# Routing weights ahead of the low halves: reordering the approach to a mixture of experts

## The chip, the cores and the metric

The kernel runs on one core of one Trainium2 chip. The metric is the device time of one execution in microseconds (us), lower is better; it is given as the median of repeated runs. A profile is one execution recorded by the hardware profiler, with a time of its own.

## The reference, cut to what matters

A two-layer block (pooling mixer, sliding window attention, two feed-forward nets) is followed by a second block with attention, an mLSTM, a gating unit and then a hierarchical mixture of experts. The change lies where the second block's mixer ends and its experts begin. There the model has 256 tokens of width 1024, 32 experts in 4 groups and 2 experts for each token:

```
h = h + hierarchical_moe(rms_norm_2(h, norm2_g), ...)

g_logits = xt @ rg_w + rg_b;  g_top = argmax(g_logits);  g_w = softmax(g_logits)[g_top]
e_in = (xt @ re_w + re_b).reshape(-1, 4, 8)[g_top]
e_val, e_loc = top_k(e_in, 2);  e_w = softmax(e_val) * g_w
y = sum over the two chosen experts of e_w * ((silu(x @ w_gate[e]) * (x @ w_up[e])) @ w_down[e])

gate = sigmoid(rms_norm_2(h, ple_norm_g) @ ple_gate_w)
h = h + gate * (p @ ple_proj_w)
```

The product `p @ ple_proj_w` depends on nothing before it.

## The kernel before, in words

Every engine has its own hand-written instruction list, and the lists meet only at semaphores. An engine runs its list strictly in order, so an instruction that waits holds all that stands behind it. Activations lie transposed, 8 chunks of 128 channels by 256 tokens. Exact products of float32 are made from a high and a low half.

The stretch in question runs in this order:

1. **norm2.** ScalarE squares the 8 chunks of the residual `hs` (line 774, `square`), GpSimd adds the first seven up in `sqsum` (lines 623 and 627, `sum_chunks`), TensorE sums over partitions (line 1382), ScalarE makes the reciprocal root (lines 780 and 781) and VectorE writes the normed chunks into `mix` (line 2004). `square_at` says where a square is kept: for norm2 in `mix`, eight places, so that no square waits for a place. `sq` has four places, and there a square k waits until square k - 4 has been summed.
2. **Router.** TensorE makes the 36 logits of each token (line 1795) and transposes the normed tokens (line 1801). ScalarE copies the transposes out as the high halves `h2h` (line 1205), and later VectorE makes the low halves `h2l` from them (line 2121, four subtractions).
3. **Routing.** VectorE works through `routing` (lines 2092 to 2147): group, two experts of each token as one-hot rows, TensorE counts ranks with them (lines 1820 to 1824), and VectorE turns ranks into slots and slots into the selection matrix `psel[0]` (lines 2154 and 2157). The two softmaxes need an exponential each, made by ScalarE (lines 1208 and 1214); VectorE waits for both with `route_exp` and computes the weights w1 and w2 in five small operations (lines 2140 to 2144).
4. **The independent product.** TensorE makes the 8 chunks of `p @ ple_proj_w` (line 1813, `per_layer`) in two banks of PSUM that alternate. ScalarE copies each out (line 1211, into `ppT`), and TensorE may write chunk c only when chunk c - 2 has been copied. Two of the chunks stand ahead of the rank matmuls and six behind; the second exponential stands behind the second copy.
5. **Gathers.** TensorE gathers the tokens of a pair of teams by `psel` (lines 1832 and 1833, `gather`), ScalarE and VectorE copy the result out (lines 1220 and 2509, `gathered`) and only then gather(1) may begin, since it writes the same two banks.
6. **Spread.** GpSimd builds eight diagonal matrices `diag` (line 759) over the room of the weights of step 4, from the slots (pairs 0 and 2) and from w1 and w2 (pairs 1 and 3). TensorE spreads them over all partitions (line 1928), ScalarE copies (line 1241), and the experts begin.
7. **Experts.** 16 teams of two experts: gate and up (line 1860), a gather for two teams later, transposes, combination of the previous team (line 1883) and down (line 1874). The weights come through six slots of `wring`, each loaded again when TensorE has used it (line 564, on SyncE's queue).

`stay_busy` (line 1292) issues matmuls whose result nobody reads.

Of the kernel before, what the change touches and what calls it, by code (L numbers as in the profile page):

```python
# [9 lines left out]
ACT = mybir.ActivationFunctionType  # L10
ALU = mybir.AluOpType
AX = mybir.AxisListType
# [4 lines left out]
KD = D // P  # L17
# [70 lines left out]
NORM, SQ0 = {}, {}  # L88
# [72 lines left out]
def bass_two_blocks(nc, a, out):  # L161
# [4 lines left out]
    with ctx:  # L166
        def sb(name, shape, dt=F32, within=None):
            return (within or ctx).enter_context(nc.sbuf_tensor(name, shape, dt))
# [3 lines left out]
        def sem(name):  # L172
            if name not in sems:
                sems[name] = ctx.enter_context(nc.semaphore(name))
            return sems[name]
# [20 lines left out]
        mix = sb("mix", [P, KD, T])  # L196
        rstd = sb("rstd", [P, 2, T])
        sq = sb("sq", [P, 4, T])
# [11 lines left out]
        small = sb("small", [P, 420])  # L210
# [167 lines left out]
        def square_at(name, c):  # L378

            if name == "mixpost0":  # L380
                return gained[:, c, :]
            return mix[:, c, :] if name in ("mixpre0", "pre1", "norm1", "norm2", "ple") or name.startswith("ffnpre") else sq[:, (SQ0[name] + c) % 4, :]

        def r_of(name):
            return rstd[:, NORM[name] % 2, :]
# [25 lines left out]
        for part in SPLIT:  # L411
            if part in THIRD:
                k = 2
            elif part in FOURTH:
                k = 3
            else:
                k, turn_of = turn_of, 1 - turn_of
# [254 lines left out]
        def _(pool):  # L672
            chain = Chain(pool, "pool_chain")
# [78 lines left out]
            pool.wait_ge(sem("y_split"), 9)  # L752
            pool.memset(zero, 0.0).then_inc(sem("diag_ready"), 1)
            pool.wait_ge(sem("pp_psum"), KD)
            for known, pairs in ((1, ((0, 160), (2, 162))), (2, ((1, 164), (3, 166)))):
                pool.wait_ge(sem("columns_ready"), known)
                for i, col in pairs:
                    for b in range(NB):
                        pool.tensor_scalar(diag[:, 2 * i + b, :], ident, small[:, col + b:col + b + 1], None, ALU.mult)\
                            .then_inc(sem("diag_ready"), 1)  # L760
# [4 lines left out]
        def square(act, name, c, src, n, rows=P, **kw):  # L765

            k = SQ0[name] + c
            if k >= 4 and name not in ("mixpre0", "mixpost0", "pre1", "norm1", "norm2", "ple") and not name.startswith("ffnpre"):
                owner_, at = next((x, k - 4 - SQ0[x]) for x, m in NORMS if k - 4 - SQ0[x] < m)
                if at < SUMMED.get(owner_, 0):  # L770
                    act.wait_ge(sem("sq_summed"), sums(owner_, at))
                else:
                    act.wait_ge(sem("sq_used"), k - 3)
            act.activation(square_at(name, c)[0:rows, 0:n], src, ACT.Square, **kw).then_inc(sem("sq_ready"), 1)  # L774
# [173 lines left out]
        def _(act):  # L948
            chain = Chain(act, "act_chain")
# [259 lines left out]
            for c in range(KD):  # L1209
                act.wait_ge(sem("pp_psum"), c + 1)  # L1210
                act.activation(ppT[:, c, :], ps[:, 6 + c % 2, 0:SEQ], ACT.Copy).then_inc(sem("pp_ready"), 1)
                if c == 1:
                    act.wait_ge(sem("route_d"), 1)
                    act.activation(small[:, 180:182], small[:, 180:182], ACT.Exp).then_inc(sem("route_exp"), 1)
            act.preload_act_table_set("silu_and_others")

            def gathered(n):
# [70 lines left out]
        def stay_busy(pe, bank, n, of=cst):  # L1288

            weights, moving = of[:, 0:P // 2].bitcast(BF16), of[:, 0:min(SEQ, of.shape[1])].bitcast(BF16)  # L1290
            for _ in range(n):
                pe.matmul(ps[:, bank, 0:moving.shape[1]], weights, moving, start=True, stop=True)
# [71 lines left out]
        def _(pe):  # L1364
# [440 lines left out]
            pe.wait_ge(sem("proj_loaded"), 16)  # L1805
            wp = wproj[:, 0:2048].rearrange("p (k n) -> p k n", k=2)
            pt = wproj[:, 2048:2560].rearrange("p (k t) -> p k t", k=2)

            def per_layer(c):
                if c >= 2:  # L1810
                    pe.wait_ge(sem("pp_ready"), c - 1)
                for k in range(2):
                    ins = mm(ps[:, 6 + c % 2, 0:SEQ], wp[:, k, c * P:(c + 1) * P], pt[:, k, :], start=(k == 0), stop=(k == 1))
                ins.then_inc(sem("pp_psum"), 1)

            for c in range(2):
                per_layer(c)
            pe.wait_ge(sem("onehot_ready"), 1)
            oh = onehot
            mm(ps[:, 5, 0:NE], C("strict"), oh(2)[:, 0, :], start=True, stop=True)  # L1820
# [1 line left out]
            mm(ps[:, 5, NE:2 * NE], C("strict"), oh(2)[:, 1, :], start=False, stop=True)  # L1822
            mm(ps[:, 5, 2 * NE:3 * NE], ones[:, :], oh(2)[:, 0, :], start=True, stop=False)
            mm(ps[:, 5, 2 * NE:3 * NE], ones[:, :], oh(2)[:, 1, :], start=False, stop=True).then_inc(sem("rank_psum"), 1)
            for c in range(2, KD):
                per_layer(c)

            def pick(out, c, select):

# [59 lines left out]
            def extra():  # L1889
                with pe.If(busiest(pe) > FEW):  # L1890
                    for evacuated in ("y_ready", "y_low"):
                        pe.wait_ge(sem(evacuated), 2 * TEAMS)
                    with pe.Fori(0, OVER_TURNS) as turn:
# [18 lines left out]
                        over.wait("dve", "y")  # L1912
                        combine((yx,), combx).then_inc(sem("over_pe"), 1)

            pe.wait_ge(sem("h2h_ready"), 4)
            pe.wait_ge(sem("h2l_ready"), 4)
            pe.wait_ge(sem("diag_ready"), 1)
            for c in range(4):
                mm(ps[:, c, :], zero[:, 0:P // 2].bitcast(BF16), zero.bitcast(BF16), start=True, stop=False, skip_group_check=True)
            pe.wait_ge(sem("pp_ready"), KD)  # L1920
            pe.wait_ge(sem("psel_ready"), 1)
            gather(0)
            for evacuated in ("xb_ready", "xb_ready_d"):
                pe.wait_ge(sem(evacuated), 1)
            gather(1)
            pe.wait_ge(sem("diag_ready"), 9)
            for q, bank in enumerate((4, 7)):
                mm(ps[:, bank, :], ones[:, :], diag[:, 4 * q:4 * q + 4, :].rearrange("p a n -> p (a n)"), start=True, stop=True)\
                    .then_inc(sem("spread_psum"), 1)
# [142 lines left out]
        def routing(dve, chain):  # L2072
# [13 lines left out]
            gl = small[:, 128:136].rearrange("p (b n) -> p b n", b=NB)  # L2086
            gmax, gsum, v1, v2, rec = (small[:, 140 + 2 * i:142 + 2 * i] for i in range(5))
            at, w1, w2 = small[:, 160:164], small[:, 164:166], small[:, 166:168]
            rank, base = small[:, 184:188], small[:, 188:192]
            ex = small[:, 180:182]  # L2090
# [24 lines left out]
            for i in range(2):  # L2115
                chain(dve.tensor_tensor(key, onehot(i), ranks[:, 0:NE].unsqueeze(1).to_broadcast([P, NB, NE]), ALU.mult))
                chain(dve.tensor_reduce(base[:, 2 * i:2 * i + 2], key, AX.X, ALU.add))
            for q in range(4):
                dve.wait_ge(sem("h2h_ready"), q + 1)
                part = slice(q % 2 * 512, (q % 2 + 1) * 512)  # L2120
                dve.tensor_tensor(h2l[:, q // 2, part], ps[:, 1 + q, :], h2h[:, q // 2, part].bitcast(F32), ALU.subtract)\
                   .then_inc(sem("h2l_ready"), 1)
# [13 lines left out]
            select(dve, chain, psel[0], 168, iota[:, :]).then_inc(sem("psel_ready"), 1)  # L2136
            dve.tensor_copy(at, small[:, 168:172]).then_inc(sem("columns_ready"), 1)
            dve.tensor_copy(route_i[:, :], many[:, 0:1]).then_inc(sem("route_ready"), 1)
            dve.wait_ge(sem("route_exp"), 2)
            chain(dve.tensor_reduce(gsum, gl, AX.X, ALU.add))  # L2140
            chain(dve.tensor_scalar(rec, ex, 1.0, None, ALU.add))
            chain(dve.tensor_tensor(rec, rec, gsum, ALU.mult))
            chain(dve.reciprocal(w1, rec))
            dve.tensor_tensor(w2, ex, w1, ALU.mult).then_inc(sem("columns_ready"), 1)
            dve.tensor_copy(small[:, 176:177], ranks[:, NE + ROUNDS - 1:NE + ROUNDS])
            chain(dve.tensor_scalar(small[:, 177:178], ranks[:, NE + ROUNDS - 1:NE + ROUNDS], float(TEAMS * P), None, ALU.add))
            chain(dve.tensor_scalar(small[:, 172:176], small[:, 168:172], float(-TEAMS * P), None, ALU.add))
# [595 lines left out]
```

## Time and profile before

| | |
|---|---|
| median of 3 runs | 1011.59 us (1008.24 to 1011.84) |
| the profiled execution | 1011.84 us, its span 1010.1 us |
| TensorE busy | 961.2 us (95%) |
| VectorE, ScalarE, GpSimd busy | 530.8, 413.9, 200.2 us |
| granted TensorE clock, mean | 0.974 of full speed |

The span is the time from the first to the last instruction. The three runs of the same kernel lie 3.6 us apart. In the rows below, PE is TensorE's matmuls, PEld its weight loads, DVE VectorE, ACT ScalarE and POOL GpSimd; L1390 is line 1390 of the kernel. A matmul of plain float32 appears in the rows as two.

### The profile page before, as it was taken

What the parts mean: (1) busy time and instruction counts of PE and PEld (TensorE: products, weight loads), DVE (VectorE), ACT (ScalarE), POOL (GpSimd) and SP (SyncE); (2) the same over time, 40 slices, a digit from 0 to 9 for tenths busy, and PEclk for the clock granted to TensorE, in tenths of its full rate; (3) what the DMA queues carried; (4) which work ended last, traced back from release to release, by engine and by line L of the source; (5) the groups of instructions that cost most, each with busy time, mean ns of one, the idle gap of its engine ahead of it and who ended that gap; (6) DMA issues with size and microseconds to landing.
All of it is one profiled execution on the core that took longest, in us unless ns stands there. A gap on an engine that the chain in (4) does not pass through costs nothing.

```text
span 1010.1 us, 16759 instructions
## 1 busy us (share of the span) xinstructions
PE 961.2 (95%) x6865; PEld 800.0 (79%) x6865; DVE 530.8 (53%) x927; ACT 413.9 (41%) x688; POOL 200.2 (20%) x266
## 2 busy tenths in 40 slices
PE   6999999999889999999999999989899999999986
PEld 5799999998777899999998999778745544554465
DVE  3745554337874755554447638763723333233366
ACT  4533333446555743334456456743311111111172
POOL 4243333112000533333112422202200000000013
PEclk8999999999899999999999999988899999999998
DMA  7444453468701444444463421127569999999911
GB/s 306 168 168 166 166 182 122 172 200 220 188 9 77 167 146 188 166 151 160 173 240 152 184 114 48 48 83 303 214 242 418 419 421 420 421 420 422 420 59 43
DMA packets 37213, 211.76 MB, mean 210 GB/s; under 512 B 2576, under 2 KB 16160, under 8 KB 18080
## 3 DMA queue, kind: packets, MB, share of 16 engines
q1 hardware_dynamic: 37152, 210.91, 54.7%
q8 instruction: 43, 0.70, 0.3%
q14 instruction: 18, 0.15, 0.0%
HBM read 209.83 MB, written 1.07 MB: 209 GB/s over the span
## 4 chain that ended last, share of the span: by engine, by line
PE 80%; DVE 13%; ACT 3%; issue 2%; POOL 1%; DMA 1%; SPq 0%; POOLq 0%; DVEq 0%; ACTq 0%
PE ps L1390 47%; PE ps L1860 11%; PE ps L1874 6%; PE ps L1883 3%; DVE mix L2004 2%; PE ps L1832 2%; DVE hs L609 2%; PE ps L1833 1%; DVE wl L809 1%; PE ps L1382 1%; PE ps L1407 1%; DMA ring<-in_w_pool 1%; PE ps L1326 1%; PE ps L1795 1%; POOL sqsum L627 1%
## 5 line engine op out<-in xcount | busy, mean ns | idle before, releaser
L809 DVE TENSOR_TENSOR wl<-ring,wh 128x2048 fp32r<-128x2048 f32 (+3 forms) x104 | 206.0, 1982 | 179.6 <-ACT wh L799 179.5
L799 ACT ACTIVATE wh<-ring 128x2048 fp32r<-128x2048 f32 (+3 forms) x104 | 172.3, 1660 | 259.6 <-PE ps L1390 257.6
L1390 PE MATMUL ps<-xh,wh 128*128 128x256 f32 (+3 forms) x600 | 171.8, 286 | 1.1 <-DVE xl L2468 1.0
L1390 PE MATMUL ps<-xh,wl 128*128 128x256 f32 (+3 forms) x600 | 170.1, 284 | 0.0
L1390 PE MATMUL ps<-xl,wh 128*128 128x256 f32 (+3 forms) x600 | 169.9, 283 | 0.0
L1390 PEld LDWEIGHTS ps<-xh,wh 128*128 128x128 f32 (+3 forms) x600 | 112.2, 187 | 2.7 <-DVE xl L2468 1.2
L1390 PEld LDWEIGHTS ps<-xh,wl 128*128 128x128 f32 (+3 forms) x600 | 112.3, 187 | 0.1
L1390 PEld LDWEIGHTS ps<-xl,wh 128*128 128x128 f32 (+3 forms) x600 | 112.3, 187 | 0.0
L1390 PE MATMUL ps<-acth,wh 128*128 128x272 f32 (+1 forms) x352 | 100.3, 285 | 0.0
L1390 PE MATMUL ps<-acth,wl 128*128 128x272 f32 (+1 forms) x352 | 100.0, 284 | 0.0
L1390 PE MATMUL ps<-actl,wh 128*128 128x272 f32 (+1 forms) x352 | 99.8, 284 | 0.0
L1390 PE MATMUL ps<-xhT,wh 128*128 128x272 f32 x320 | 92.2, 288 | 0.0
L1390 PE MATMUL ps<-xhT,wl 128*128 128x272 f32 x320 | 92.1, 288 | 0.0
L1390 PE MATMUL ps<-xlT,wh 128*128 128x272 f32 x320 | 92.1, 288 | 0.0
L648 POOL TENSOR_TENSOR mix<-mix 128x272 f32<-128x272 f32 (+1 forms) x44 | 36.8, 835 | 155.7 <-DVE mix L2032 140.4
L623 POOL TENSOR_TENSOR sqsum<-mix 128x256 f32<-128x256 f32 (+1 forms) x7 | 6.3, 899 | 308.8 <-ACT mix L774 308.8
L1390 PEld LDWEIGHTS ps<-acth,wh 128*128 128x128 f32 x352 | 66.3, 188 | 0.0
L1390 PEld LDWEIGHTS ps<-acth,wl 128*128 128x128 f32 x352 | 66.2, 188 | 0.0
L1390 PEld LDWEIGHTS ps<-actl,wh 128*128 128x128 f32 x352 | 66.1, 188 | 0.0
L2560 DVE TENSOR_TENSOR yl<-ps,yh 128x512 fp32r<-128x512 f32 x32 | 20.6, 686 | 86.3 <-ACT yh L1256 86.3
L1390 PEld LDWEIGHTS ps<-xhT,wl 128*128 128x128 f32 x320 | 60.2, 188 | 0.0
L1390 PEld LDWEIGHTS ps<-xhT,wh 128*128 128x128 f32 x320 | 60.1, 188 | 0.0
(450 smaller groups left out, 1928.6 us busy)
## 6 DMA issues: line engine op xcount, KB each, us to landing
wring<-in_w_eg SPq DMA_DIRECT2D x32, 2048.0 KB, 13.2
ring<-in_w_gu SPq DMA_DIRECT2D x22, 2048.0 KB, 7.4
wring<-in_w_ed SPq DMA_DIRECT2D x16, 2048.0 KB, 11.5
ring<-in_w_dn SPq DMA_DIRECT2D x16, 1408.0 KB, 5.9
ring<-in_w_z SPq DMA_DIRECT2D x7, 2048.0 KB, 7.4
ring<-in_w_out SPq DMA_DIRECT2D x4, 1152.0 KB, 5.2
ring<-in_w_q SPq DMA_DIRECT2D x8, 512.0 KB, 6.0
ring<-in_w_o SPq DMA_DIRECT2D x8, 512.0 KB, 15.4
```

The lines of the kernel that those rows point to most:

```text
L609: eng.tensor_tensor(hs[:, c, cols], hs[:, c, cols], mix[:, c, 0:n], ALU.add).then_inc(hs_add(c), 1)
L627: pool.tensor_tensor(total, total, square_at(name, c)[:, 0:n], ALU.add).then_inc(sem("sq_summed"), 1)
L648: pool.tensor_tensor(mix[:, 6 + j, 0:n], mix[:, 2 + j, 0:n], mix[:, 4 + j, 0:n], ALU.mult)\
L799: ins = act.activation(to, src, ACT.Copy)
L809: ins = dve.tensor_tensor(to, src, h.bitcast(F32), ALU.subtract)
L1390: ins = mm(o, p, q, start=first and n == 0, stop=last and n == 2)
L1832: mm(out, h2h[:, k, at], select[:, k, :], start=(k == 0), stop=False)
L1860: ins = mm(ps[rows, 4, :], x[:, k, rows], chunk(slot)[:, j, i * 512:(i + 1) * 512], start=(k == 0), stop=(k == KD - 1))
L1874: ins = mm(ps[rows, 6 + i, :], heT[:, k, rows], chunk(slot)[:, j, k * D + i * 512:k * D + (i + 1) * 512], start=(k == 0), stop=(k == 1))
L1883: ins = mm(ps[:, c // 2, c % 2 * SEQ:(c % 2 + 1) * SEQ], y[:, c * P:(c + 1) * P], weights, start=False, stop=last and y is parts[-1], skip ...
L2004: return dve.scalar_tensor_tensor(dst, src, V(name, c), r, ALU.mult, ALU.mult)
L2560: dve.tensor_tensor(yl[:, i * 512:(i + 1) * 512], ps[:, 6 + i, :], yh[:, i * 512:(i + 1) * 512].bitcast(F32), ALU.subtract).then_inc(sem(" ...
```

## The change

Five edits, all between norm2 and the experts:

- norm2's squares are kept in `sq` and no longer in `mix`, so squares 4 to 7 wait for GpSimd's sums of squares 0 to 3.
- TensorE makes all 8 chunks of the independent product before the rank matmuls. ScalarE makes the second exponential behind the eighth copy, no longer behind the second.
- VectorE waits for both exponentials and computes w1 and w2 ahead of the low halves `h2l`, no longer behind `psel[0]`.
- GpSimd builds the diagonals of the weights first and those of the slots second. Each pair still follows the semaphore of its own columns.
- TensorE issues 11 more matmuls of `stay_busy` ahead of the gathers, and waits for the eighth copy behind gather(1), no longer ahead of gather(0).

```diff
 def square_at(name, c):
-            return mix[:, c, :] if name in ("mixpre0", "pre1", "norm1", "norm2", "ple") or name.startswith("ffnpre") else sq[:, (SQ0[name] + c) % 4, :]
+            return mix[:, c, :] if name in ("mixpre0", "pre1", "norm1", "ple") or name.startswith("ffnpre") else sq[:, (SQ0[name] + c) % 4, :]
...
 # GpSimd
-            for known, pairs in ((1, ((0, 160), (2, 162))), (2, ((1, 164), (3, 166)))):
+            for known, pairs in ((1, ((1, 164), (3, 166))), (2, ((0, 160), (2, 162)))):
                 pool.wait_ge(sem("columns_ready"), known)
...
 # ScalarE
-            if k >= 4 and name not in ("mixpre0", "mixpost0", "pre1", "norm1", "norm2", "ple") and not name.startswith("ffnpre"):
+            if k >= 4 and name not in ("mixpre0", "mixpost0", "pre1", "norm1", "ple") and not name.startswith("ffnpre"):
...
             for c in range(KD):
                 act.wait_ge(sem("pp_psum"), c + 1)
                 act.activation(ppT[:, c, :], ps[:, 6 + c % 2, 0:SEQ], ACT.Copy).then_inc(sem("pp_ready"), 1)
-                if c == 1:
-                    act.wait_ge(sem("route_d"), 1)
-                    act.activation(small[:, 180:182], small[:, 180:182], ACT.Exp).then_inc(sem("route_exp"), 1)
+            act.wait_ge(sem("route_d"), 1)
+            act.activation(small[:, 180:182], small[:, 180:182], ACT.Exp).then_inc(sem("route_exp"), 1)
...
 # TensorE
-            for c in range(2):
-                per_layer(c)
+            for c in range(KD):
+                per_layer(c)      # written out in place
             pe.wait_ge(sem("onehot_ready"), 1)
             ...                   # the rank matmuls
-            for c in range(2, KD):
-                per_layer(c)
...
+            stay_busy(pe, 0, 11)
             pe.wait_ge(sem("h2h_ready"), 4)
             pe.wait_ge(sem("h2l_ready"), 4)
             ...                   # zeros the four banks of the sum
-            pe.wait_ge(sem("pp_ready"), KD)
             pe.wait_ge(sem("psel_ready"), 1)
             gather(0)
             for evacuated in ("xb_ready", "xb_ready_d"):
                 pe.wait_ge(sem(evacuated), 1)
             gather(1)
             pe.wait_ge(sem("diag_ready"), 9)
+            pe.wait_ge(sem("pp_ready"), KD)
...
 # VectorE, routing()
+            dve.wait_ge(sem("route_exp"), 2)
+            ...                   # gsum, rec, w1, w2, then columns_ready
             for q in range(4):
                 dve.wait_ge(sem("h2h_ready"), q + 1)
                 ...               # the low halves h2l
             ...                   # ranks, slots, psel[0], columns_ready, route_ready
-            dve.wait_ge(sem("route_exp"), 2)
-            ...                   # gsum, rec, w1, w2, then columns_ready
```

## Rows read from the trace of the kernel before

**Rows 1.** The page, the chain of work that ended last, shares by engine.
```profile
PE 80%; DVE 13%; ACT 3%; issue 2%; POOL 1%; DMA 1%; SPq 0%; POOLq 0%; DVEq 0%; ACTq 0%
```

**Rows 2.** Stretches: length, busy us of each engine, granted clock, DMA share, GB/s.
```profile
711.00:718.00 7.00, 7.00 (x35) 6.97 (x35) 3.12 (x17) 1.97 (x4) 0.00 (x0) 0.51 1.01 420
718.00:731.00 13.00, 10.93 (x62) 9.10 (x60) 11.97 (x45) 5.57 (x13) 4.17 (x7) 1.00 0.15 62
731.00:735.00 4.00, 3.92 (x17) 3.59 (x18) 0.45 (x1) 0.60 (x1) 0.91 (x2) 0.57 0.00 0
737.00:950.00 213.00, 211.15 (x1167) 105.69 (x1167) 70.12 (x177) 34.86 (x72) 0.00 (x0) 1.00 0.99 408
985.00:1010.00 25.00, 15.01 (x116) 13.66 (x114) 17.44 (x33) 6.06 (x13) 9.53 (x11) 0.82 0.13 43
```

**Rows 3.** Timeline of ScalarE: start us, length us, instruction, idle before it.
```profile
719.63 0.38 ACT L1211 ACTIVATE work<-ps 128x256 f32<-128x256 f32 x1 [0.48 <-PE ps L1813]
719.91 0.20 ACT L1214 ACTIVATE small<-small 128x2 f32<-128x2 f32 x1
722.07 0.38 ACT L1211 ACTIVATE work<-ps 128x256 f32<-128x256 f32 x1 [1.97 <-PE ps L1813]
...
726.39 0.38 ACT L1211 ACTIVATE work<-ps 128x256 f32<-128x256 f32 x1 [0.48 <-PE ps L1813]
```

**Rows 4.** Timeline of VectorE through the routing.
```profile
720.49 0.22 DVE L2117 TENSOR_REDUCE small<-work 128x2 f32<-128x64 f32 x1
720.74 2.48 DVE L2121 TENSOR_TENSOR h2l<-ps,h2h 128x512 fp32r<-128x512 f32 x4
723.14 0.18 DVE L2125 TENSOR_REDUCE work<-ps 128x1 f32<-128x32 f32 x1
...
725.05 0.62 DVE L2154 TENSOR_SCALAR psel<-iota,small 128x256 fp32r<-128x256 f32 x2
725.70 0.88 DVE L2157 SCALAR_TENSOR_TENSOR psel<-iota,small,psel 128x256 fp32r<-128x256 f32 x2
...
726.63 0.15 DVE L2140 TENSOR_REDUCE small<-small 128x2 f32<-128x8 f32 x1
...
727.56 0.14 DVE L2145 COPY small<-ranks 128x1 f32<-128x1 f32 x1
...
728.45 0.73 DVE L2154 TENSOR_SCALAR psel<-iota,small 128x256 fp32r<-128x256 f32 x2
...
730.24 0.69 DVE L2509 COPY xb_even<-ps 128x512 f32<-128x512 f32 x1
```

**Rows 5.** Timeline of TensorE through the product, the gathers and the first expert.
```profile
717.58 2.01 PE L1813 MATMUL ps<-work 128*128 128x256 f32 x8
...
720.93 5.43 PE L1813 MATMUL ps<-work 128*128 128x256 f32 x24
726.19 1.03 PE L1919 MATMUL ps<-work 128*128 128x512 bf16 x4
726.87 0.47 PE L1832 MATMUL ps<-psel,h2h 128*128 128x256 f32 x1
...
731.08 0.36 PE L1832 MATMUL ps<-psel,h2h 128*128 128x256 f32 x1 [1.96 <-DVE xb_even L2509]
...
737.16 7.09 PE L1860 MATMUL ps<-wring,xb_even 128*64 128x512 f32 x32 [0.69 <-ACT work L1241]
```

**Rows 6.** Timeline of GpSimd: norm2's sums, and the diagonals.
```profile
699.24 1.23 POOL L623 TENSOR_TENSOR sqsum<-mix 128x256 f32<-128x256 f32 x1 [36.52 <-ACT mix L774]
...
701.81 3.33 POOL L627 TENSOR_TENSOR sqsum<-sqsum,mix 128x256 f32<-128x256 f32 x4 [0.46 <-ACT mix L774]
...
726.83 5.08 POOL L759 TENSOR_SCALAR work<-cst,small 128x128 f32<-128x128 f32 x8 [21.44 <-DVE small L2137]
```

**Rows 7.** Timeline of ScalarE, norm2's squares 0 to 4 and 7.
```profile
698.38 1.63 ACT L774 ACTIVATE mix<-hs 128x256 f32<-128x256 f32 x5
...
704.14 0.42 ACT L774 ACTIVATE mix<-hs 128x256 f32<-128x256 f32 x1 [2.77 <-DVE hs L2499]
```

More of the change, by code:

```diff
@@ L1807, in _ @@
             pt = wproj[:, 2048:2560].rearrange("p (k t) -> p k t", k=2)
-            def per_layer(c):
+            for c in range(KD):
                 if c >= 2:
@@ L2117, in routing @@
                 chain(dve.tensor_reduce(base[:, 2 * i:2 * i + 2], key, AX.X, ALU.add))
+            dve.wait_ge(sem("route_exp"), 2)
+            chain(dve.tensor_reduce(gsum, gl, AX.X, ALU.add))
+            chain(dve.tensor_scalar(rec, ex, 1.0, None, ALU.add))
+            chain(dve.tensor_tensor(rec, rec, gsum, ALU.mult))
+            chain(dve.reciprocal(w1, rec))
+            dve.tensor_tensor(w2, ex, w1, ALU.mult).then_inc(sem("columns_ready"), 1)
             for q in range(4):
@@ L2138, in routing @@
             dve.tensor_copy(route_i[:, :], many[:, 0:1]).then_inc(sem("route_ready"), 1)
-            dve.wait_ge(sem("route_exp"), 2)
[L2140 to L2144, printed above, removed]
             dve.tensor_copy(small[:, 176:177], ranks[:, NE + ROUNDS - 1:NE + ROUNDS])
```

## Prediction

> **What bounds the kernel now.** I read the page's chain of work first. It lies on TensorE for 80% and on VectorE for 13% [rows 1]; the reader should see that an edit counts only if it moves TensorE, or if it lies where TensorE waits for VectorE. Next come the stretches [rows 2]. From 737 to 950 us TensorE is busy for 211.15 of 213 us at a full clock of 1.00: the experts run without gaps, and whatever moves their start moves the end by as much. So the question is when the first expert matmul starts, 737.16 us here [rows 5]. The chain in front of it, in order of time, runs through VectorE: low halves, ranks, `psel[0]`, then `psel[1]`, the copy of gather(0) at 730.24, and only then gather(1) at 731.08, after TensorE had idled for 1.96 us [rows 4, 5]. VectorE is busy for 11.97 of the 13 us from 718 to 731, TensorE for 10.93 [rows 2]. VectorE's list bounds this stretch, and the timelines of each engine give the terms.
>
> **The change part by part.**
>
> The second exponential. Before, it starts at 719.91 behind the second copy. Now it stands behind the eighth. The copies of six chunks in a row come (726.39 - 722.07) / 5 = 0.864 us apart, at TensorE's pace, since ScalarE idles 0.48 us before them [rows 3]. The second copy stays at 719.63, as nothing ahead of them changes. The rank matmuls no longer part the second from the third, so the eighth copy starts at 719.63 + 6 x 0.864 = 724.81. The exponential follows 0.28 us later (719.91 - 719.63) and takes 0.20 us, which gives 725.29; with about 0.05 us for the handover, an estimate, VectorE is released at 725.34.
>
> VectorE's wait. It now asks for that exponential behind the last reduction before the low halves, which ends at 720.49 + 0.22 = 720.71 [rows 4]. It stands still for 725.34 - 720.71 = 4.63 us. Queued behind it are the low halves, the ranks, `psel[0]` and `psel[1]`; TensorE waits for all of them.
>
> The weights. Five operations take 727.56 - 726.63 = 0.93 us [rows 4]. They now come first, so the low halves start at 725.34 + 0.93 = 726.27, which is 5.53 us later than 720.74. Behind `psel[0]` the 0.93 us are given back. `psel[0]` ends at 725.70 + 0.88 + 5.53 = 732.11, and gather(0), which started 0.29 us after it, starts at 732.40. The copy of gather(0) can be taken by VectorE at 730.24 + 5.53 - 0.93 = 734.84, so gather(1) and the first expert come 5.53 - 0.93 = 4.60 us later.
>
> The rank matmuls, moved behind the product, have no price. The eight-matmul group started at 717.58 and its successor starts at most 720.93 - 719.59 = 1.34 us after its end with the ranks in between [rows 5]. Without them the product ends near 717.58 + 8 x 0.864 = 724.5, and with them the ranks are there by 725.9. VectorE asks for them only at 723.14 + 5.53 = 728.67, the late low halves covering them. If VectorE did not stall, it would ask at 723.14 and the same move would cost 2.7 us: the cover is the stall itself.
>
> The 11 matmuls of `stay_busy`. Four of the same width start from 726.19 and the next instruction follows by 726.87 to 727.2, so one takes 0.17 to 0.26 us [rows 5], 11 take 1.9 to 2.9 us. They start at 725.9 and end by 728.8, while TensorE may not go on before the low halves are whole at 726.27 + 2.40 = 728.67. They cost nothing, or 0.1 us ahead of a gather that is itself not due before 732.40.
>
> The wait for the eighth copy, moved behind gather(1): that copy is over at 725.2 and gather(0) starts at 732.40, so it binds in neither place. Zero.
>
> GpSimd's order. The eight diagonals took 5.08 us from 726.83 [rows 6], 0.64 us each. Now four start when w1 and w2 are there, 726.3, and end by 728.8; four start behind `psel[0]`, at about 732.2, and end at 734.8. gather(1) ends after 737.6, so the spread does not wait. Without that cover it would cost nothing until 737.6. There is a side effect, since four diagonals now run beside the low halves: no row shows those two together. The nearest rows are line 2154's pairs, 0.62 us before GpSimd starts and 0.73 us beside it [rows 4, 6], 0.11 us more. For four subtractions that bounds it at +0.4 us; below, it is nothing, since four diagonals fewer stand beside other work of VectorE. I take 0, as the subtractions read PSUM where those pairs read SBUF alone, and keep 0.4 for the range.
>
> norm2's squares. Square 4 must wait for the sum of 0 and 1, over at 699.24 + 1.23 = 700.47, and so ends near 701.0 where it ended at 700.0 [rows 6, 7]. Squares 5 and 6 follow at ScalarE's pace of a third of a us (1.63 for five), the last of them behind the sum of square 2, which is over before 701.81, so by about 702.2. GpSimd takes squares 3 to 6 from 701.81 on at 3.33 / 4 = 0.83 us each, square 4 at 702.6 and square 6 at 703.5 or later. The last square waits for `hs` until 704.14 in any case. The slack is 1.3 us or more, and the cost nothing; were it gone, each late square would add up to its 0.42 us. A few waits more on ScalarE ahead of the first sum: 0 to 0.1 us.
>
> The sum: 4.60 + 0 = 4.6 us later. The profiled execution took 1011.84 us, 1.74 us of it outside its span, so 1016.4 us. That execution is the slowest of the three, 0.25 us above their median.
>
> **The clock.** From 731 to 735 us the granted clock is 0.57, that is mostly 1.2 in place of 2.4 GHz, right after the idle 1.96 us, and there gather(1) runs [rows 2, 5]. It lost 4.00 x 0.43 = 1.7 us. In the new order TensorE idles about 2.5 us before gather(0) and 1.2 us or so before gather(1), so the low clock could reach back to gather(0). I take the same loss as before, the nearest row. Bounds: no low clock at all, -1.7 us; all of gather(0), gather(1) and the spread at half clock: gather(0) then takes 2 x 1.8 = 3.6 us from 732.40, over at 736.0 where VectorE could copy at 734.84, +1.2 us, and the rest another +1.4 us. The Trainium skill ("TensorE: Matmul & The Clock Gate", Part 1) says that the throttled state is the default and that activity releases it. By that rule the 11 matmuls would keep the clock up only if no idle time came behind them, and here it does; the trace agrees so far as the low stretch at 731 follows an idle one.
>
> **The rivals.**
>
> (a) Colder clock: the stall as above, and gather(0) at half clock as well, or the clock returning later than 718 us, where the product now paces the exponential and thus VectorE. For it: the low stretch from 711 to 718 (0.51) ends just as the product begins [rows 2], and before there was slack on TensorE's side that is now gone. Against: one execution shows neither. It gives 4.6 + 1.2 to 2.6, some 1018.2 us.
>
> (b) Warmer clock: the filler holds it and gather(1) runs at 2.4 GHz. It gives 4.6 - 1.7 = 2.9, or 1014.7 us.
>
> (c) No stall, because the exponential is there when VectorE asks, or because what is lost is taken back among the experts. For it: the weights of the experts come in at a DMA share of 0.99 [rows 2], and were they the bound, a late start could be caught up. Against: TensorE has 1.85 us idle in 213, and the slots are loaded again only when TensorE has used them, so the loads start later too. 1011.8 us.
>
> (d) Faster, by the clock behind the experts: from 985 to 1010 the clock is 0.82, a loss of 4.5 us, and from 711 to 718 it is 0.51, a loss of 3.4 us [rows 2]. If the new timing gave both back, and the 1.7 us of gather(1), the kernel would end 9.6 - 4.6 = 5.0 us earlier, 1006.8 us. It decides once more than 4.6 us of lost clock come back; it is slower before that. Nothing in the change touches these places, which speaks against it; that runs of one kernel lie 3.6 us apart speaks for some such play.
>
> **How the numbers follow.** The forecast has 0.46, (a) 0.27, (b) 0.14, (c) 0.06, (d) 0.07. The predicted time is 1016.4 us. The range: below, the fastest run of before with the warm clock, 1008.24 + 2.9 = 1011.1; above, 1011.84 + 4.6 + 2.6 + 0.4 = 1019.4. That takes in (a), (b), (c) in part, and leaves out most of (d) and half of (c). What a measurement of this kernel can tell from no change is about 0.5%, 5.1 us, that is 1016.6 us above. My forecast stands just inside: of its 0.46 I give 0.15 to slower and 0.31 to the same. Slower: 0.15 + 0.27 = 0.42. The same: 0.31 + 0.14 + 0.06, and 0.01 of (d), 0.52. Faster: 0.06.
>
> **What would show it.** VectorE idles some 4.6 us ahead of the first of its five weight operations, released by ScalarE's small exponential; that one starts near 724.8 to 725.1, behind eight copies 0.86 us apart. The low halves start near 726.3 and the first expert matmul near 741.8, with the experts then 14.7 us a team as before. norm2's sums keep their times, and the diagonals end before gather(1) does. I am wrong if VectorE shows no such idle time, if the experts show waits for DMA, or if the granted clock around the gathers differs from 0.57 by much.

## The result, and the profile after

The changed kernel takes 1014.63 us in the median of 7 runs (1010.49 to 1016.55). The kernel before takes 1008.40 us in 7 runs, four of them taken beside it (1006.01 to 1011.84). The ratio is 1.0052 with a 95% interval of 1.0033 to 1.0072, so the change costs about 5.2 us, and between 3.3 and 7.3. The two medians lie 6.2 us apart, inside the same interval. Measured twice more beside other kernels, it is 1.0063 (1.0046 to 1.0080) and 1.0050 (1.0031 to 1.0069). The profiled execution takes 1016.52 us with a span of 1014.8, against 1011.84 and 1010.1.

The chain of work that ended last, on the page of the changed kernel, answers to [rows 1]:

```profile
PE 83%; DVE 10%; ACT 3%; issue 2%; DMA 1%; POOL 1%; SPq 0%; DVEq 0%; POOLq 0%; ACTq 0%
```

VectorE's share of the chain fell from 13% to 10% although VectorE stands still for longer. The chain follows releases: from 704.03 to 724.20 us it now lies on TensorE without a break (norm2's sum, router, transposes, product), then it goes over the eighth copy and the small exponential to VectorE. Before, it lay on VectorE's list from the router's end at 714.37 on. A wait is booked on what ends it, so a late engine can lose share.

Stretches of the changed kernel, columns as in [rows 2]:

```profile
704.00:711.00 7.00, 6.97 (x32) 4.84 (x32) 3.26 (x8) 0.80 (x2) 0.14 (x1) 0.76 1.01 422
711.00:718.00 7.00, 7.00 (x32) 6.64 (x32) 4.35 (x22) 2.48 (x5) 0.00 (x0) 0.51 1.01 419
718.00:731.00 13.00, 10.59 (x54) 7.61 (x52) 6.94 (x28) 4.44 (x10) 2.36 (x4) 1.00 0.05 20
731.00:735.00 4.00, 3.47 (x16) 3.38 (x16) 2.81 (x12) 0.60 (x1) 2.68 (x4) 0.58 0.00 0
735.00:742.00 7.00, 5.37 (x27) 3.07 (x28) 2.66 (x6) 1.79 (x3) 0.00 (x0) 0.99 0.01 2
742.00:955.00 213.00, 211.31 (x1174) 106.67 (x1171) 68.84 (x175) 35.08 (x72) 0.00 (x0) 1.00 0.99 411
```

From 718 to 731 VectorE is busy for 6.94 us where it was busy for 11.97. The experts run as before, 211.31 of 213 us busy at a full clock: nothing is caught up there.

Timeline of ScalarE, the product's copies and the exponential, answering to [rows 3]:

```profile
718.13 0.38 ACT L1211 ACTIVATE work<-ps 128x256 f32<-128x256 f32 x1 [1.01 <-PE ps L1811]
719.02 0.38 ACT L1211 ACTIVATE work<-ps 128x256 f32<-128x256 f32 x1 [0.51 <-PE ps L1811]
...
724.20 0.38 ACT L1211 ACTIVATE work<-ps 128x256 f32<-128x256 f32 x1 [0.48 <-PE ps L1811]
724.48 0.20 ACT L1213 ACTIVATE small<-small 128x2 f32<-128x2 f32 x1
```

Timeline of VectorE, answering to [rows 4] (here line 2106 is the last one-hot sum, 2113 the first of the five weight operations, 2122 the low halves, 2152 the end of a selection, 2504 the copy of gather(0)):

```profile
718.10 0.22 DVE L2106 TENSOR_TENSOR small<-small 128x64 f32<-128x64 f32 x1
...
719.08 0.22 DVE L2111 TENSOR_REDUCE small<-work 128x2 f32<-128x64 f32 x1
724.78 0.16 DVE L2113 TENSOR_REDUCE small<-small 128x2 f32<-128x8 f32 x1 [5.48 <-ACT small L1213]
...
725.65 2.48 DVE L2122 TENSOR_TENSOR h2l<-ps,h2h 128x512 fp32r<-128x512 f32 x4
728.04 0.18 DVE L2126 TENSOR_REDUCE work<-ps 128x1 f32<-128x32 f32 x1
...
730.60 0.88 DVE L2152 SCALAR_TENSOR_TENSOR psel<-iota,small,psel 128x256 fp32r<-128x256 f32 x2
...
733.07 0.88 DVE L2152 SCALAR_TENSOR_TENSOR psel<-iota,small,psel 128x256 fp32r<-128x256 f32 x2
735.32 0.69 DVE L2504 COPY xb_even<-ps 128x512 f32<-128x512 f32 x1 [1.37 <-PE ps L1826]
```

The stall is there: 5.48 us of idle time, ended by the small exponential. A second, smaller one stands ahead of the copy of gather(0), 1.37 us, ended by TensorE.

Timeline of TensorE, answering to [rows 5] (product, ranks' last, filler, zeroing, gather(0), gather(1), first expert):

```profile
716.18 7.99 PE L1811 MATMUL ps<-work 128*128 128x256 f32 x32
...
724.81 0.39 PE L1819 MATMUL ps<-small,ones 128*128 128x32 f32 x2
725.03 2.54 PE L1291 MATMUL ps<-cst 128*128 128x512 bf16 x11
728.23 1.02 PE L1913 MATMUL ps<-work 128*128 128x512 bf16 x4 [0.66 <-issue]
731.53 0.48 PE L1825 MATMUL ps<-psel,h2h 128*128 128x256 f32 x1 [2.28 <-DVE psel L2152]
...
736.16 0.35 PE L1825 MATMUL ps<-psel,h2h 128*128 128x256 f32 x1 [0.94 <-DVE xb_even L2504]
...
740.71 7.09 PE L1853 MATMUL ps<-wring,xb_even 128*64 128x512 f32 x32 [0.69 <-ACT work L1240]
```

Timeline of GpSimd, answering to [rows 6]:

```profile
725.90 2.36 POOL L759 TENSOR_SCALAR work<-cst,small 128x128 f32<-128x128 f32 x4 [21.77 <-DVE small L2117]
731.65 2.68 POOL L759 TENSOR_SCALAR work<-cst,small 128x128 f32<-128x128 f32 x4 [3.39 <-DVE small L2138]
```

To compare kernels whose earlier stretches differ by their clock, I read each one from VectorE's last one-hot sum on. In the kernel before that sum starts here:

```profile
719.51 0.22 DVE L2112 TENSOR_TENSOR small<-small 128x64 f32<-128x64 f32 x1
```

The table splits the way to the first expert matmul into A, from that sum to the low halves; B, on to the end of `psel[0]`; C, on to VectorE's copy of gather(0); and D, from gather(1) to the first expert matmul. 0.83 to 0.84 us lie between C and D in all of them. Each row is one profiled execution.

| kernel | A | B | C | D | total |
|---|---|---|---|---|---|
| before | 1.23 | 5.84 | 3.66 | 6.08 | 17.65 |
| changed | 7.55 | 5.83 | 3.84 | 4.55 | 22.61 |
| changed, second | 7.27 | 5.83 | 3.77 | 4.55 | 22.26 |
| changed, third | 7.22 | 5.82 | 3.75 | 4.54 | 22.16 |
| early exponential | 2.10 | 5.96 | 2.60 | 4.55 | 16.05 |
| exponential back alone | 2.10 | 7.17 | 2.51 | 4.55 | 17.16 |
| no filler | 6.24 | 5.83 | 3.94 | 6.49 | 23.34 |
| filler at gather(0) | 6.12 | 5.83 | 2.51 | 4.54 | 19.84 |
| squares in `mix` | 7.66 | 5.82 | 3.76 | 4.55 | 22.63 |
| late exponential alone | 1.23 | 5.83 | 3.67 | 6.08 | 17.65 |
| product first alone | 1.24 | 9.52 | 3.73 | 4.54 | 19.87 |
| `psel[1]` later | 1.23 | 5.83 | 3.24 | 4.55 | 15.69 |
| the same with filler | 1.23 | 5.84 | 2.82 | 4.55 | 15.28 |
| `psel[1]` later, zeroing earlier | 1.22 | 5.84 | 2.68 | 4.64 | 15.21 |

For the pair before and changed the total grows by 4.96 us: A +6.32, B 0, C +0.18, D -1.53. The spans differ by 4.7: the one-hot sum itself came 1.41 us earlier in the changed execution, and what follows the first expert matmul took 1.15 us longer (274.09 against 272.94). The second profile of the changed kernel took 273.04 there, so the 1.15 us are no property of the change.

### The profile page after: what moved, and what is told of

The parts are those of the page before. It is cut to its first block, busy times and chain, and to the rows that moved or that the text cites. A ratio compares the mean times of both kernels' runs of the same rounds, so it can differ in the third digit from the quotient of the medians.

```text
span 1014.8 us, 16789 instructions
## 1 busy us (share of the span) xinstructions
PE 961.9 (95%) x6876; PEld 797.9 (79%) x6876; DVE 530.3 (52%) x927; ACT 413.8 (41%) x688; POOL 200.0 (20%) x266
## 4 chain that ended last, share of the span: by engine, by line
PE 83%; DVE 10%; ACT 3%; issue 2%; DMA 1%; POOL 1%; SPq 0%; DVEq 0%; POOLq 0%; ACTq 0%
PE ps L1389 48%; PE ps L1853 11%; PE ps L1867 6%; PE ps L1876 3%; DVE mix L1998 2%; PE ps L1825 2%; DVE hs L609 2%; PE ps L1826 2%; PE ps L1381 1%; DVE wl L809 1%; PE ps L1406 1%; PE ps L1811 1%; PE ps L1325 1%; DMA ring<-in_w_pool 1%; POOL sqsum L627 1%
## 5 line engine op out<-in xcount | busy, mean ns | idle before, releaser
L1389 PE MATMUL ps<-xh,wh 128*128 128x256 f32 (+3 forms) x600 | 169.5, 282 | 2.4 <-DVE wl L809 1.3
L1389 PE MATMUL ps<-xh,wl 128*128 128x256 f32 (+3 forms) x600 | 167.8, 280 | 0.0
L1389 PE MATMUL ps<-xl,wh 128*128 128x256 f32 (+3 forms) x600 | 167.8, 280 | 0.0
L1389 PEld LDWEIGHTS ps<-xh,wh 128*128 128x128 f32 (+3 forms) x600 | 109.9, 183 | 4.3 <-DVE wl L809 1.5
L1389 PEld LDWEIGHTS ps<-xh,wl 128*128 128x128 f32 (+3 forms) x600 | 110.0, 183 | 0.1
L1389 PEld LDWEIGHTS ps<-xl,wh 128*128 128x128 f32 (+3 forms) x600 | 110.0, 183 | 0.0
L1389 PEld LDWEIGHTS ps<-xlT,wh 128*128 128x128 f32 x320 | 60.1, 188 | 0.0
```

Source lines behind the costliest of these rows:

```text
L1389: ins = mm(o, p, q, start=first and n == 0, stop=last and n == 2)
```

## The experiments

Theory: the loss is VectorE standing still for an exponential that ScalarE reaches last, because its wait was moved ahead of everything that TensorE needs. Rivals: the new order costs by itself; the clock; the waits of the squares; the late ranks.

### Early exponential

```diff
-            act.wait_ge(sem("route_d"), 1)          # behind the eighth copy
-            act.activation(small[:, 180:182], ..., ACT.Exp)
+                if c == 1:                          # behind the second
+                    act.wait_ge(sem("route_d"), 1)
+                    act.activation(small[:, 180:182], ..., ACT.Exp)
...
-            for c in range(KD): per_layer(c)
+            for c in range(2): per_layer(c)         # the other six behind the ranks
-            stay_busy(pe, 0, 11)
```

The wait for the eighth copy stands ahead of gather(0) again. VectorE's and GpSimd's order and the squares stay changed.

> VectorE's order, GpSimd's order and norm2's squares as in the changed kernel; the exponential stands behind the second copy again, the product is split 2 + 6, and the 11 filler matmuls are out. Theory (the whole loss is VectorE standing still for an exponential that ScalarE makes last): no stall ahead of the weights, low halves start 0.93 us later than before, psel[0] ends at 727.5, and since the 0.93 us are given back behind psel[0] the first expert is where it was: within 0.5 us of the kernel before, so 4.6 us or more below the changed kernel. Rival (the order of VectorE and GpSimd costs by itself): still 1 us or more above the kernel before, with no stall to show for it.

Measured: 1.0008 (0.9994 to 1.0021). In its profile no wait stands ahead of the weights, the low halves start 0.87 us later than before after the one-hot sum (A 2.10), and C is 1.06 us shorter (2.60). Its total of 16.05 lies 0.1 us from that of the kernel before with gather(1) at full clock, 17.65 - 1.53 = 16.12. So in this stretch the order of VectorE and GpSimd costs nothing that shows; the loss is gone with the late exponential and the late ranks. The time alone does not settle it: the medians are 1.75 us apart (1009.31 and 1007.56), and the interval, -0.6 to +2.1 us, does not exclude the rival's 1 us.

### No filler, squares in `mix`, and the changed kernel again

```diff
-            stay_busy(pe, 0, 11)
```

> The changed kernel without its 11 filler matmuls. Theory (the filler lies wholly in TensorE's wait for the low halves and idle time follows it, so that it neither costs nor keeps the clock up): 0 to 0.5 us against the changed kernel, gather(0) still starts 0.3 us behind psel[0]. Rival (the filler holds the clock): gather(0), gather(1) and the spread at half clock, 1.4 us or more above the changed kernel.

```diff
-            return mix[:, c, :] if name in (..., "norm1", "ple") ...
+            return mix[:, c, :] if name in (..., "norm1", "norm2", "ple") ...
```

> The changed kernel with norm2's squares back in mix. Theory (GpSimd's sums set the pace and the squares have slack): the four squares in a row become five, GpSimd's sums start and end as before, 0 us against the changed kernel within noise. Rival (the waits for a place in sq cost): 0.4 us or more below the changed kernel, and GpSimd's sums ending that much earlier after the last residual addition.

> The changed kernel as it is, on the same chip as the three beside it: 4.6 us above the kernel before from the stall alone, up to 6 where gather(0) falls into the half clock.

Measured on one chip: without filler 1.0071 (1.0054 to 1.0088), squares in `mix` 1.0059 (1.0037 to 1.0080), the changed kernel 1.0063 (1.0046 to 1.0080). The times do not tell these three apart. Their profiles do.

The squares cost nothing. Timelines of ScalarE and of GpSimd in the changed kernel:

```profile
697.13 1.32 ACT L774 ACTIVATE sq<-hs 128x256 f32<-128x256 f32 x4
699.30 0.73 ACT L774 ACTIVATE sq<-hs 128x256 f32<-128x256 f32 x2 [0.85 <-POOL sqsum L623]
```

```profile
697.98 1.22 POOL L623 TENSOR_TENSOR sqsum<-sq 128x256 f32<-128x256 f32 x1 [33.71 <-ACT sq L774]
699.35 0.74 POOL L627 TENSOR_TENSOR sqsum<-sqsum,sq 128x256 f32<-128x256 f32 x1
700.55 3.34 POOL L627 TENSOR_TENSOR sqsum<-sqsum,sq 128x256 f32<-128x256 f32 x4 [0.46 <-POOL sqsum L627]
```

ScalarE waits 0.85 us for a place, but the sums run as in [rows 6]: 5.91 us from the first one's start to the last one's end, where it was 5.90. In the kernel with the squares back in `mix` ScalarE makes five squares in a row and the sums take 5.91 us as well (700.89 to 706.80).

The filler is a different matter. It does not lengthen the way, but without it TensorE idles from the ranks to the zeroing, and the clock is low from about 725.3 us, inside that wait, until 738.9. With it, in the changed profile, it stayed at 2.4 GHz until 731.7, when gather(0) had begun. TensorE, then the stretches, of the kernel without filler:

```profile
726.98 1.49 PE L1912 MATMUL ps<-work 128*128 128x512 bf16 x3 [3.41 <-issue]
```

```profile
725.00:730.00 5.00, 1.58 (x4) 0.53 (x5) 4.69 (x20) 0.00 (x0) 1.64 (x3) 0.53 0.00 2
730.00:735.00 5.00, 4.06 (x18) 3.79 (x19) 2.87 (x9) 0.60 (x1) 2.69 (x4) 0.50 0.00 0
735.00:741.00 6.00, 5.43 (x20) 3.90 (x19) 0.69 (x1) 1.72 (x3) 0.00 (x0) 0.67 0.00 0
```

From the low halves on (B, C and D) it takes 2.1 us more than the second changed profile: 17.10 against 14.99, the gap between C and D included. The theory's "0 to 0.5 us" fell; the rival's 1.4 us or more held for this stretch. That the total grew by 1.08 us only is because A was 1.03 us shorter in that execution. The mean clock of its six runs (0.974 to 0.977, where the changed kernel's beside it have 0.977 to 0.985) points the same way.

### Filler right ahead of gather(0)

```diff
+            stay_busy(pe, 4, 10)
             pe.wait_ge(sem("psel_ready"), 1)
             gather(0)
```

> The changed kernel with 10 more filler matmuls of 512 columns in a free bank, right ahead of gather(0), where TensorE waited 2.28 us for psel[0]. Theory (in the changed kernel the stall costs about 5 us by VectorE's list and another 1.4 us because gather(0) runs at half clock after that wait, so that VectorE waits for it): clock 1.00 from there to the first expert, VectorE's copy of gather(0) with no idle time ahead of it, 1.2 to 1.5 us below the changed kernel. Rival (the half clock at gather(0) costs nothing, VectorE's list is longer anyway): same as the changed kernel within 0.5 us, or above it where the filler delays gather(0).

> The changed kernel as it is, on the chip of the two beside it, as their base: 5 to 6.5 us above the kernel before.

Measured on one chip: 1.0046 (1.0029 to 1.0063) against the changed kernel's 1.0050 (1.0031 to 1.0069). The profile with the filler:

```profile
724.00:738.00 14.00, 11.41 (x62) 6.73 (x62) 9.50 (x32) 2.90 (x5) 5.06 (x8) 1.00 0.01 2
```

```profile
732.52 0.69 DVE L2505 COPY xb_even<-ps 128x512 f32<-128x512 f32 x1
```

The clock is full from 724 to the first expert, the wait of VectorE ahead of the copy is gone, and C falls from 3.75 to 2.51, by 1.24 us, as expected. The median moved by 0.4 us, within the intervals, so the gain is shown in the profile and not in the time.

### The exponential back alone

The changed kernel with the exponential behind the second copy (the ScalarE part of the first diff) and the wait for the eighth copy ahead of gather(0); product, ranks, weights and filler as changed.

> The changed kernel with the exponential behind the second copy again; the product still comes before the ranks, and VectorE still makes the weights first. Theory (the stall covers the late ranks): VectorE does not wait for the exponential, but for the ranks behind its low halves, 2.7 to 3.6 us less the 0.93 us of the weights that now stand ahead, so 1.8 to 2.7 us; psel[0] is 2.7 to 3.6 us later than before and the time some 2 us below the changed kernel, not at that of before. Rival (the exponential is all): the time of the kernel before within 1 us.

Measured: 1.0013 (0.9996 to 1.0029), 3.4 us below the changed kernel beside it (1009.94 against 1013.32). VectorE:

```profile
724.20 0.19 DVE L2127 TENSOR_REDUCE work<-ps 128x1 f32<-128x32 f32 x1 [1.25 <-PE ps L1820]
```

The wait went where the theory put it, from the exponential to the ranks, but it was 1.25 us and not 1.8 to 2.7. The product was early here: its second copy came 0.39 us ahead of the one-hot sum (717.99 and 718.38). `psel[0]` is 2.2 us late against the one-hot sum. The total, 17.16, lies 1.1 us above the early exponential's. By time the rival ("within 1 us of before") is as near as the theory; the row decides for the theory in kind, with a smaller size.

### One edit at a time in the kernel before

```diff
                 act.activation(ppT[:, c, :], ..., ACT.Copy)
-                if c == 1:
-                    act.wait_ge(sem("route_d"), 1)
-                    act.activation(small[:, 180:182], ..., ACT.Exp)
+            act.wait_ge(sem("route_d"), 1)
+            act.activation(small[:, 180:182], ..., ACT.Exp)
```

> The kernel before with one edit: the exponential behind the eighth copy; VectorE still asks for it behind psel[0]. Theory (a late exponential costs only where it is asked for early): it ends near 726.9 and VectorE asks at 726.63, so +0.3 us at the first expert, the same time within noise. Rival (ScalarE's order costs by itself, whoever asks): 2 us or more above the kernel before.

```diff
-            for c in range(2):
+            for c in range(KD):
                 per_layer(c)
             ...                                     # the rank matmuls
-            for c in range(2, KD):
-                per_layer(c)
```

> The kernel before with one edit: TensorE makes all eight chunks of the product before the rank matmuls; the exponential stays behind the second copy. Theory (in the changed kernel the late ranks are hidden by the stall alone): the ranks are there at 725.9 and VectorE asks at 723.14, so VectorE stands still for 2.7 us behind its low halves and the first expert comes 2.7 us later. Rival (the ranks are early enough wherever they stand): same as before, VectorE idle for under 0.5 us.

Measured: late exponential alone 1.0007 (0.9990 to 1.0023), its total 17.65 as before; product first alone 1.0045 (1.0028 to 1.0061). The first says that a late exponential is harmless as long as VectorE does not ask for it early; there VectorE waited 0.19 us for it. The second cost more than the 2.7 us expected. VectorE there, behind its low halves:

```profile
717.02 2.48 DVE L2119 TENSOR_TENSOR h2l<-ps,h2h 128x512 fp32r<-128x512 f32 x4
723.10 0.19 DVE L2123 TENSOR_REDUCE work<-ps 128x1 f32<-128x32 f32 x1 [3.60 <-PE ps L1824]
```

3.60 us of waiting for the ranks, 0.9 more than worked out. Here the product's second copy came 1.10 us after the one-hot sum (716.88 and 715.78), before it had come 0.12 us after. That difference of 0.98 us accounts for the excess: at the offset of before the wait would have been 2.6 us. The total in the table is only 2.2 us above that of before, where the time says 4.5 (2.8 to 6.2); the section on the prediction comes back to this.

### Towards a faster kernel

`psel[1]` is read by gather(2) alone, yet VectorE makes it before it copies gather(0).

```diff
-            selected(1)
             gathered(0)
             gathered(1)
+            selected(1)
```

> The kernel before with one edit: VectorE makes psel[1], which only gather(2) reads, behind its two copies of the gathers and no longer ahead of the first. Theory (VectorE's list bounds gather(1)): the copy of gather(0) starts near 729.2 in place of 730.24 and gather(1) 1.1 us earlier; with TensorE idle for 0.9 us in place of 1.96 the low clock may stay away too, 1.7 us more. 1.1 to 2.8 us below the kernel before. Rival (GpSimd's diagonals, done at 731.9, or the spread bound the start of the experts): 0 to 0.5 us below, TensorE waiting for GpSimd ahead of the spread.

> As the kernel beside it, with 5 filler matmuls of 512 columns in a free bank between gather(0) and gather(1), about 1.1 us, in the time that TensorE waits for the copies. Theory (the half clock follows idle time at the gathers, and a filler with no idle time behind it prevents it): granted clock 1.00 from gather(0) to the first expert, 2.3 to 2.8 us below the kernel before and no more than 0.3 us above the kernel beside it. Rival (the clock falls for what lies further back, or the filler delays gather(1)): clock near 0.57 there as before, and the time as without the filler or up to 1 us more.

And on top of the first, the zeroing, with the three waits ahead of it, moved ahead of the product's last two chunks, and `pe.wait_ge(sem("pp_ready"), KD - 1)` ahead of gather(0):

> The kernel before with psel[1] made behind both copies, the four zeroing matmuls moved ahead of the product's last two chunks, and gather(0) waiting for the seventh copy only. Theory (with psel[1] out of the way, gather(0) waits for TensorE's own product, the zeroing and the last copy, 0.84 us behind psel[0]): gather(0) starts within 0.2 us of psel[0], the first expert 14.5 to 15.0 us behind the last one-hot sum where the kernel with the one edit had 15.69, 1 to 2 us below the kernel before. Rival (the stretch is bound elsewhere by now, or the clock takes back what is won): under 0.5 us below the kernel before.

Measured: 0.9987 (0.9969 to 1.0006), with filler 0.9995 (0.9979 to 1.0011), with the zeroing earlier 0.9988 (0.9973 to 1.0004). The profiles have the first expert 2.0 to 2.4 us sooner than the profile of before; of this 1.5 us are the clock of gather(1) (D 4.55 in place of 6.08) and 0.4 to 1.0 us are C. The copy of gather(0) now waits for TensorE, here in the first version:

```profile
725.18 0.69 DVE L2509 COPY xb_even<-ps 128x512 f32<-128x512 f32 x1 [1.82 <-PE ps L1833]
```

So neither theory held in full: VectorE's list no longer bounds gather(1), but TensorE's product and gather(0) do, 0.4 to 1 us earlier. gather(0) starts 0.84 us behind the end of `psel[0]` in the first version, 0.43 with the filler and 0.29 with the zeroing earlier, and C is 2.39 to 2.40 us plus that delay in all three. The kernel before had 0.29 too; at that delay C would be 2.68, which is 0.98 us below its 3.66 and close to the 1.04 worked out. What differs is again the product, whose second copy came 1.13 us behind the one-hot sum in the first version. So the earlier zeroing shows no gain of its own, and missed both its marks (0.2 us behind `psel[0]`, first expert at 14.5 to 15.0; measured 0.29 and 15.21). The filler shows none either: the clock was full from gather(0) to the first expert with it, as expected, and also without it, and the time did not fall by 2.3 to 2.8 us. No version is shown to beat the kernel before; a gain of 0.1% is what the medians hint at and the intervals do not confirm.

## Why the prediction was right

The forecast was 1016.4 us, +4.6 on the profiled execution, inside the range that was given; measured are 1014.63 us and a ratio that stands for +5.2. The prediction gave more to "the same" than to "slower" because it took 0.5% as what a measurement can tell; the interval of 1.0033 to 1.0072 lies wholly above no change. The mechanism is the forecast one. By its steps:

- **Exponential behind the eighth copy.** Copies 0.863 us apart (719.02 to 724.20), worked out 0.864. Right.
- **VectorE's wait.** 4.63 us worked out, 5.48 in the profile, 5.15 in the third profile, 4.05 in the one with filler at gather(0). The size hangs on when the product starts at full speed against VectorE's one-hots. In all six profiles that have this wait it is 4.56 us plus the distance from the last one-hot sum to the second copy: 0.92 us in the changed profile, 0.59 in the third, -0.51 with filler at gather(0). Before, the distance was 0.12, and the prediction let it stay. So of this wait only that distance was off, by 0.80 us. That part of case (a), the product now pacing VectorE, is borne out.
- **The weights.** 0.87 us (724.78 to 725.65), given back behind `psel[0]`. Right, the early exponential shows it alone.
- **The ranks.** Hidden, as said: asked for at 728.04, done by 725.2. The price without the cover was put at 2.7; it measured 3.60 alone and 1.25 behind the weights. Less the distance to the second copy (1.10 and -0.39) these are 2.50 and 1.64, apart by the 0.87 us of the weights. Right in kind, and at the distance of before, 0.12, also in size: 2.6.
- **The filler.** Its 2.54 us cost nothing. But the sentence that it could not keep the clock up because idle time follows was wrong by half: without it B, C and D took 2.1 us more. The idle times behind the filler, 0.66 and 2.28 us, brought the low clock only at gather(0).
- **The eighth copy's wait, GpSimd's order, norm2's squares.** Nothing, as said. The low halves took 2.48 us beside the diagonals and 2.48 without them [rows 4], so the 0.4 us kept for contention were not needed. The Trainium skill ("SBUF — State Buffer", Who interferes with whom) says that a VectorE instruction with at most one input in SBUF, outside the modes that use both port pairs, does not contend with GpSimd. The trace agrees for the low halves, whose other input is in PSUM.
- **The clock.** "The same loss as before" came out right in sum and wrong in place. gather(1) and the spread ran at full clock, -1.53 us in D. gather(0) ran at half clock and VectorE waited 1.37 us for it, as case (a) said with 1.2.

The sum by measured terms is 4.60 + 0.79 (A beyond the forecast 5.53) + 1.37 (gather(0)) - 1.53 (gather(1)) - 0.26 (small operations and `psel[1]`, which ran that much shorter; that GpSimd stood beside all of them before is a likely reason, not a shown one) = 4.97, against 4.96 read. Two clock effects of 1.4 and 1.5 us cancelled, and that the forecast met the profile this closely owes something to that. So does the time of 1016.4: it is built on an execution that proved the slowest of seven, 3.4 us above their median.

How often gather(1) of the kernel before runs at half clock is open. Both profiles of kernels with its order there did, and unprofiled runs show no clock by stretch. The times speak against its being the rule. Measured from the 17.65 us of before, five totals of the table lie outside the intervals of their times:

| kernel | total less 17.65 | total less 16.12 | measured, us |
|---|---|---|---|
| early exponential | -1.6 | -0.1 | -0.6 to +2.1 |
| exponential back alone | -0.5 | +1.0 | -0.4 to +2.9 |
| product first alone | +2.2 | +3.8 | +2.8 to +6.2 |
| filler at gather(0) | +2.2 | +3.7 | +2.9 to +6.3 |
| `psel[1]` later, with filler | -2.4 | -0.8 | -2.1 to +1.1 |

Measured from 16.12, the same way with gather(1) and the spread at full clock, every kernel of the table lies inside its interval. This is an argument and no proof, since each total is that of one execution. By it the changed kernel is typically 6.0 to 6.5 us slower, and the half clock at gather(1) is no usual part of the kernel before. The two profiles that have it took 1011.84 and 1011.34 us, where the medians of their kernels are 1008.40 and 1009.87.

## What to carry to other kernels

In an in-order engine a wait costs by what stands behind it, not by what it waits for: the same late exponential cost nothing that shows where it was asked for last and 5.5 us of waiting where it was asked for first. Price a moved operation together with the cover it had, since one that is free under a stall (the ranks) costs up to 3.6 us once the stall is gone. Where several stages hand over to each other, read the distance between two marks inside the trace beside the total time. In the three profiles of the changed kernel B, C and D repeat within 0.1 us where repeated runs spread over 5. But choose the marks so that no change of the clock lies between them: A contains one, and it ranged from 6.12 to 7.66 us under edits that do not touch it. And a profile is one execution, so check against the times whether its clock is the usual one.

## What the runs showed of the hardware

The clock granted to TensorE fell not only after idle time. From 711 to 718 us it is 0.51 in both kernels while TensorE is busy for all of the 7.00 us: the router's matmuls with 36 moving columns run there, then the transposes. In all fourteen profiles it fell while the router ran, and it was back at 2.4 GHz between 0.6 us ahead of the product's start and 2.3 us behind it. That is the spread that moved VectorE's wait.

Nor did idle time of one length always have one effect. Ahead of norm2's sum over partitions TensorE waited 1.63 us in the kernel before and 1.62 us in the changed one. In the first the clock stayed at 2.4 GHz up to 711 us, in the second it was at 1.2 GHz from about 704.4 to 707.8 us. The kernel before, then the changed one, whose stretch from 704 to 711 stands above with 0.76:

```profile
705.28 0.67 PE L1382 MATMUL ps<-sqsum,ones 128*128 128x256 f32 x2 [1.63 <-POOL sqsum L627]
704.00:711.00 7.00, 5.14 (x26) 3.55 (x26) 3.36 (x9) 1.22 (x3) 1.25 (x3) 1.00 1.01 422
```

```profile
704.03 0.87 PE L1381 MATMUL ps<-sqsum,ones 128*128 128x256 f32 x2 [1.62 <-POOL sqsum L627]
```

In the kernel without filler the clock fell inside a wait of 3.41 us and stayed at 1.2 GHz for some 13.6 us, gathers included that kept TensorE busy for 4.06 of 5 us. The Trainium skill ("TensorE: Matmul & The Clock Gate", Part 1) says that the throttled clock is the default and that sustained activity releases it. The traces agree in that the clock came back under work and, in the kernel without filler, left in idle time; that a stretch recorded as fully busy can lose the clock as well is what the busy share alone would have hidden.
